# A hybrid decoder step on one core: the state-space input projected first, keys, values and queries beside the state scan

## The reference, cut to what matters

```python
h = rmsnorm(x, g)                      # 1032 tokens together
z = h @ w_in                           # queries 512 | keys/values of three branches 768 | gates 24 | u 512
nsa = gates * (compressed + selected + window attention)   # 8 heads, 2 key heads
state[t] = a * state[t-1] + B u[t]     # complex diagonal state of 32 groups x 64, 1024 steps
y = Re(C state) + d * u;  ssm = gelu(y) * sigmoid(gelu(y) @ glu_w + glu_b)
x = x + norm(concat(norm(nsa), norm(ssm)) @ w_out)
mkv = rmsnorm(mem) @ xkv               # 256 memory tokens: keys and values of the cross-attention
x = x + norm(cross_attention(x, mkv));  x = x + norm(swiglu(x))
```

## Time and profile before

| what | us |
|---|---|
| median of three runs (lowest, highest) | 2453.48 (2452.53, 2455.98) |
| the profiled execution, its own time | 2469.54 |
| its span, first to last instruction | 2467.8 |
| mean granted clock of TensorE over the span, as a share of 2.4 GHz | 0.852 |
| PE busy in the span | 2054.3 |

### The profile page before, as it was taken

One profiled execution on the slowest core, in us unless ns is written; L12 is line 12 of the kernel. 1 busy time (PEld: TensorE's weight loads), 2 busy tenths in 40 slices (PEclk: granted clock), 3 DMA queues, 4 the chain that ended last, 5 costly groups with the idle time before them and its releaser, 6 DMA issues.

```text
span 2467.8 us, 28572 instructions
## 1 busy us (share of the span) xinstructions
PE 2054.3 (83%) x11440; PEld 1758.9 (71%) x11440; DVE 1048.8 (42%) x2439; ACT 625.7 (25%) x1240; POOL 139.3 (6%) x236
## 2 busy tenths in 40 slices
PE   5989890467889889867697879949999999999994
PEld 3646570235778788654497559649999999999993
DVE  3142479939888735200524204081322313223126
ACT  3410120043344444321323113151111111111112
POOL 2100002011101000321000010000000000000000
PEclk9989995675576888966699877969999999999997
DMA  3211112024332100864030030101111111111101
GB/s 120 75 31 35 43 35 77 0 83 134 128 119 95 35 1 1 219 137 105 9 112 26 26 128 1 54 23 35 50 45 46 50 43 50 45 46 50 43 18 77
DMA packets 122547, 151.19 MB, mean 61 GB/s; under 512 B 13488, under 2 KB 104792, under 8 KB 116368
## 3 DMA queue, kind: packets, MB, share of 16 engines
q0 software_dynamic: 17392, 81.67, 10.9%
q1 hardware_dynamic: 95200, 59.91, 8.3%
q10 hardware_dynamic: 9824, 7.78, 1.0%
HBM read 137.03 MB, written 12.31 MB: 61 GB/s over the span
## 4 chain that ended last, share of the span: by engine, by line
PE 46%; DVE 5%; issue 1%; DMA 1%; ACT 1%; POOL 0%; DVEq 0%; POOLq 0%
PE PS L612 43%; PE PS L616 2%; DVE A L2338 1%; DVE A L1766 1%; ACT A L1346 1%; DMA A<-in_cache_mem_kv 1%; DMA A<-new_selected_row 0%; DVE hL L1766 0%; DVE hRaw L1766 0%; DVE A L2349 0%; DVE A L2312 0%; DVE mA L1766 0%; DMA A<-in_norm_g 0%; DVE mS L2314 0%; DVE A L2290 0%
## 5 line engine op out<-in xcount | busy, mean ns | idle before, releaser
L612 PE MATMUL PS<-A 128*128 128x64 f32 (+15 forms) x3728 | 757.7, 365 | 124.8 <-DVEq L2017 86.4
L612 PEld LDWEIGHTS PS<-A 128*128 128x128 f32 (+3 forms) x3728 | 565.8, 211 | 314.8 <-DVEq L2017 86.6
L616 PE MATMUL PS<-ident,A 128*128 128x128 f32 (+9 forms) x1528 | 288.4, 341 | 216.7 <-DVE A L2349 53.8
L616 PEld LDWEIGHTS PS<-ident,A 128*128 128x128 f32 (+9 forms) x1528 | 218.2, 170 | 270.6 <-DVE A L2349 59.8
L1346 ACT ACTIVATE A<-PS 128x256 f32<-128x256 f32 (+15 forms) x404 | 229.8, 586 | 691.6 <-PE PS L612 423.1
L1766 DVE TENSOR_TENSOR A<-A 128x1024 f32<-128x1024 f32 (+11 forms) x405 | 316.5, 785 | 11.4 <-DMA A<-in_cmp_pos 1.4
L612 PE MATMUL PS<-hH,wL 128*128 128x344 f32 x1056 | 224.3, 321 | 2.9 <-issue 2.9
L612 PE MATMUL PS<-hL,wH 128*128 128x344 f32 x1056 | 224.2, 320 | 0.0
L612 PE MATMUL PS<-hH,wH 128*128 128x344 f32 x1056 | 223.6, 320 | 0.0
L612 PEld LDWEIGHTS PS<-hH,wL 128*128 128x128 f32 x1056 | 177.4, 189 | 4.0 <-issue 4.0
L612 PEld LDWEIGHTS PS<-hL,wH 128*128 128x128 f32 x1056 | 177.6, 189 | 0.0
(11 more groups left out here) (265 smaller groups left out, 1798.6 us busy)
## 6 DMA issues: line engine op xcount, KB each, us to landing
wRaw<-in_ffn_wi SPq DMA_DIRECT2D x44, 512.0 KB, 3.8
wRaw<-in_ffn_wo SPq DMA_DIRECT2D x28, 384.0 KB, 3.1
out<-A POOLq DMA_DIRECT2D x16, 512.0 KB, 3.1
A<-in_cache_mem_kv POOLq DMA_DIRECT2D x16, 512.0 KB, 5.0
A<-in_x_prompt SPq DMA_DIRECT2D x8, 512.0 KB, 3.9
A<-in_w_in SPq DMA_DIRECT2D x8, 512.0 KB, 4.1
A<-in_xkv SPq DMA_DIRECT2D x8, 512.0 KB, 3.9
A<-bias_by_distance POOLq DMA_DIRECT2D x8, 512.0 KB, 3.9
```

Source lines behind the costliest of these rows:

```text
L612: return nc.tensor.matmul(out, lhsT=lhsT, rhs=rhs, start=start, stop=stop, skip_group_check=True)
L616: return nc.tensor.transpose(out, in_, ident[b:b + n, b:b + n])
```

## The change

It moves stages; the arithmetic stays. All nine x tiles get buffers of their own and are loaded at once; state and past parameters are issued by SP behind them (the bias table by POOL). `n1` runs for all tiles, with DVE's scaling one tile ahead of its copy. Then come `C`, `h0`, u (m 4 to 7), `SA`/`SB`. DVE's u copies are spread among the building of `CP`. SP loads `wkv` and the weights of the queries when `s5_built` and `u_moved` are set. Then PE does `kv`, `kT`, `cproj`, the queries, and only then waits for the scan; DVE does the value and product work of each kv tile (`kv_rows`) at fixed steps of the scan (`KV_AT`). `bt` units stand between V units from the ninth on; their first two loads are issued behind the kv rows. POOL's first gathers stand behind the last `bt` and `st`. The memory keys and values move behind `glu` 1, ahead of `wT`, with the load of `mem_prompt` issued by ACT at the end of the attention. ACT's list follows PE's. Arena positions are changed to fit.

```diff
+KV_AT = {4: 1, 8: 2, 13: 3, 18: 5, 22: 6, 26: 7}
...
-    order = ["par", ("n1", 0), ("n1", 1)]
-    for i in range(NT + 1):
-        order += [("kv", i)] + ([("n1", i + 2)] if i + 2 <= NT else []) + ([("kT", i - 1)] if i else [])
-    order += ["cproj", "C", "h0"]
-    order += [("in", m, c) for m in range(8) for c in range(2)]
+    order = ["par"] + [("n1", i) for i in range(NT + 1)] + ["C", "h0"]
+    order += [("in", m, c) for m in range(4, 8) for c in range(2)]
     order += [("SA", 0)]
     for j in range(NPAIR):
         order += ([("SA", j + 1)] if j + 1 < NPAIR else []) + [("SB", j)]
-    order += [("mn", i) for i in range(2)] + [("mk", c) for c in range(8)]
-    order += [("V", j) for j in range(NPAIR)]
+    for i in range(NT + 1):
+        order += [("kv", i)] + ([("kT", i - 1)] if i else [])
+    order += ["cproj"]
+    order += [("in", m, c) for m in range(4) for c in range(2)]
+    for j in range(NPAIR):
+        order += [("V", j)] + ([("bt", j - 8)] if j >= 8 else [])
     order += ["ys", "st"] + [("sst", q) for q in range(4)]
-    order += [("bt", h) for h in range(NH)]
...
+    order += [("mn", i) for i in range(2)] + [("mk", c) for c in range(8)]
...
+        for m in (4, 5, 6, 7, 0, 1, 2, 3):
             c0 = m * P if m < 4 else OFF_U + (m - 4) * P
             stream.append((wi_[:, c0:c0 + P], KD, ("in", m, 1)))
+        first_q = 4
+        first_glu = len(stream)
+        for m in range(2):
+            stream.append((glu_w[0][:, m * P:(m + 1) * P], 4, ("glu", m, 1)))
         for m in range(8):
             stream.append((xkv[0][:, m * P:(m + 1) * P], KD, ("mk", m)))
-        first_glu = len(stream)
-        for m in range(4):
...
-                if i >= 2:
-                    full(sp, ("n1", i - 2))
                 src = x_prompt[0, c0:c0 + n, :] if i < NT else x_sample[:, 0, :]
-                sp.dma_start(xin[0:n, i % 2, :], src).then_inc(x_in[i % 2], 16)
-                if i == 1:
+                sp.dma_start(xin[0:n, i, :], src).then_inc(x_in[i], 16)
...
+            def state_parameters():
...
+            def past_parameters():
...
+            for it, (src, kt, _) in enumerate(stream):
+                if it == 2:
+                    state_parameters()
+                if it == NS:
+                    past_parameters()
+                if it == first_q:
+
+                    sp.wait_ge(s5_built, 1)
+                    sp.wait_ge(u_moved, 1)
                     sp.dma_start(wkv, wi_[:, NH * HD:OFF_U].rearrange("(k p) n -> p k n", p=P)).then_inc(wkv_in, 16)
...
-
+                norm_transposes(i)
...
+            dense("in", range(4, 8), [KD], lambda k: hT[:, k])
...
+            pe.wait_ge(wkv_in, 16)
+            for i in range(NT + 1):
+                c0, n = token_tile(i)
+                s = open_(("kv", i))
...
-            for c in range(8):
-                w = next_weights()
...
+            dense("in", range(4), [KD], lambda k: hT[:, k])
...
+                    pe.wait_ge(hank_in[h % 2], 16 * (h // 2 + 1))
+                    s = open_(("bt", h))
+                    for c in range(2):
+                        ins = mm(s[:, c * 512:(c + 1) * 512], flip[:, :], hank[:, h % 2, c * 512:(c + 1) * 512])
+                    ins.then_inc(filled, 1)
             pe.wait_ge(hs_ready, 1)
             s = open_("ys")
             for j in range(NPAIR):
...
             dense("glu", range(2), [4], lambda k: yF[:, k])
 
+            for i in range(2):
...
+            def bias_rows(h):
+                pool.dma_start(hank[:, h % 2], bass.AP(bias_dram.tensor, h * VL, [[1, P], [1, T]]))\
+                    .then_inc(hank_in[h % 2], 16)
+
+            full(pool, ("kv", NT))
+            for h in range(2):
+                bias_rows(h)
...
+            for h in range(2, NH):
+                full(pool, ("bt", h - 2))
+                bias_rows(h)
+
+            full(pool, ("bt", NH - 1))
+            full(pool, "st")
             past_line(0)
...
-            full(act, ("mk", 7))
+
+            for m in range(4):
+                dense_out("in", m, qT[:, m])
             own.settle()
             f(kH, kTd).then_inc(k_hi, 1)
+            for h in range(NH):
+                full(act, ("bt", h))
...
+            full(act, ("PV", n_at - 1))
+            act.dma_start(mrow, mem_prompt[0].rearrange("(i p) d -> p i d", p=P)).then_inc(mem_in, 16)
             for m in range(2):
                 glu_out(m)
+            act.wait_ge(mem_in, 16)
...
+                full(act, ("mk", c))
+                free(f(mkv_new[:, :, c * P:(c + 1) * P], slot(("mk", c))[:, 0:256].rearrange("p (i n) -> p i n", i=2)), ("mk", c))
...
+            act.dma_start(p_mem_kv[0, 0].rearrange("(i p) c h d -> p i (c h d)", p=P), mkv_new).then_inc(mkv_out, 16)
...
+            for i in range(NT + 1):
+                if i < NT:
+                    normalise(i + 1)
+                features(i)
 
...
-            dve.wait_ge(rows_saved, 64)
+            dve.wait_ge(v8_out, 16)
...
+            def states_in(m):
...
+            states_in(0)
+            read_out(dve, "C")
+            for k in range(5):
+                if k == 3:
+                    states_in(1)
+                pw = apow[:, k]
+                cmul(halves(lambda g: CP[:, 0, :, k, 16 * g:16 * g + 16]),
...
+            for m in range(2, 4):
+                states_in(m)
...
+            def kv_rows(i):
+
+                dve.wait_ge(kv_ready, i + 1)
+                own.step(v.tensor_copy(vkeep[:, i].rearrange("p (a c) -> p a c", a=2),
+                                       kvst[:, i % 2, 256:768].rearrange("p (a b c) -> p a b c", a=2, b=2)[:, :, 1]))
+                if i >= 2:
+                    full(dve, ("kT", i - 2))
+                tt(cprod[:, i % 2], kvst[:, i % 2, 0:256], posP).then_inc(prod_ready, 1)
...
+            kv_rows(0)
             for n in range(1, 16):
                 advance(Hm[:, :, n], Hm[:, :, n - 1], 0, 16)
+                if n in KV_AT:
+                    kv_rows(KV_AT[n])
             for m in range(1, 16):
                 advance(Hm[:, m:m + 1, 15], Hm[:, m - 1:m, 15], 1, 1)
+            kv_rows(4)
             for n in range(15):
                 advance(Hm[:, 1:16, n], Hm[:, 0:15, 15], 2 + n, 15)
+                if 16 + n in KV_AT:
+                    kv_rows(KV_AT[16 + n])
 
             sb4 = [P, NPAIR, DB]
...
             dve.sem_inc(hs_ready, 1)
 
-
...
+            dve.wait_ge(kv_stored[0], 16 * (2 * 4 + 2))
+            dve.wait_ge(kv_stored[1], 16 * (2 * 4 + 2))
+            dve.wait_ge(rows_saved, 64)
```

More of the change, by code:

```diff
@@ L407, in hymba_step @@
         params = sem("params")
-        x_in = [sem(f"x_in{s}") for s in range(2)]
+        x_in = [sem(f"x_in{s}") for s in range(NT + 1)]
         wkv_in = sem("wkv_in")
@@ L711, in _ @@
             ins.then_inc(filled, 1)
-            dense("in", range(8), [KD], lambda k: hT[:, k])
+            for i in range(NT - 3, NT + 1):
+                read_out(pe, ("n1", i))
+            dense("in", range(4, 8), [KD], lambda k: hT[:, k])
             def s5_matrices(j):
@@ L1174, in _ @@
             g.memset(eps_c[:, :], EPS).then_inc(consts, 1)
+            with nc.allow_non_contiguous_dma(reason="a table of 32 by 8, transposed"):
+                pool.dma_start(tab[:, :], rel_bias.rearrange("b h -> h b")).then_inc(tab_in, 16)
             pool.wait_ge(params, 16 * PARAM_DMAS)
@@ L1435, in _ @@
-            for part, src in enumerate((state_ssm_re, state_ssm_im)):
-                act.dma_start(h0row[0:DB, part], src[0].rearrange("b g p -> b (g p)")).then_inc(c_in, 16)
-            full(act, "C")
-            for half in range(2):
-                for part in range(2):
-                    s = slot("C")[0:HD, part * 512:part * 512 + 512]\
-                        .rearrange("p (q g i) -> p q g i", g=2, i=16)[:, :, half]
-                    ins = f(cc[64 * half:64 * half + 64, part], s)
-                    free(ins, "C") if half and part else own.step(ins)
@@ L1477, in _ @@
-            act.wait_ge(s5_built, 1)
-            act.dma_start(mrow, mem_prompt[0].rearrange("(i p) d -> p i d", p=P)).then_inc(mem_in, 16)
-            for j in range(NPAIR):
-                s5_out(j)
-                if j == 8:
-                    act.wait_ge(mem_in, 16)
-                    for i in range(2):
-                        own.then(f(junk2, mrow[:, i], ACT.Square, accum_out=st[:, i:i + 1]))
-                        f(st[:, 16 + i:17 + i], st[:, i:i + 1], ACT.Sqrt, scale=1.0 / D, bias=eps_c[:, :]).then_inc(mem_stat, 1)
@@ L1507, in _ @@
             act.sem_inc(states_staged, 1)
-            for h in range(NH):
-                full(act, ("bt", h))
-                free(f(BT[:, h], slot(("bt", h))), ("bt", h))
             def softmax_rows(n, src_ready, stat, x, s, scale=SC):
@@ L2223, in _ @@
                     compressed_branch(key)
+            for i in range(2):
+                dve.wait_ge(mem_stat, i + 1)
```

(6 more changed lines are left out.)

356 lines of the change are left out of this document (159 added, 197 removed).

## The result

The changed kernel takes 2348.84 us (median of four runs, 2340.14 to 2354.44), the kernel before 2453.01 in the same comparison: a ratio of 0.9563, 95% interval 0.9541 to 0.9585. Forecast were 2344, range 2328 to 2370. The profiled execution took 2347.29 us, with a span of 2345.6 and a mean granted clock of 0.879. In the changed file the matmul helper is L651, the transposes L655, ACT's helper L1388, DVE's two-input instructions L1781.

The account below looks back on a forecast made before the run. PE was taken as busy 2054 us, its some 410 us not busy being winnable by reordering. Terms -143.4 ahead of the attention and +33.6 behind it gave -109.8: 2344 us for the median, range 2328 to 2370.

Parts of the forecast that it names:

- Step 1: Start to SA: DVE's serial list of 80.7 us sets the pace, SA at 112.7 against 282.97.
- Step 2: SA, SB, kv, queries: queries begin at 268.4, scan ends by 293 at most, V's first DVE addition at 328.0, 133.5 earlier.
- the crossing: kv and scan lists waiting for each other: costed at nothing, covered by one kv tile, only tile 4 at the edge.
- Step 3: V with bt, to the attention: 4.2 us a pair, then 21.2 us; attention starts at 395.7, 143.4 earlier.
- kL blocks V: Rival in V: `kL` on POOL holds a DVE addition, V's additions 8.6 us later, 2353; chance 0.13.
- Step 4: The attention and its 136 units: unchanged, cost nothing.
- Step 5: Memory keys moved behind the attention: `wT` at 1069.3 instead of 1035.69, 33.6 us added.
- that rival: Memory weights late behind the attention: 1.5 MB more, `mem_prompt` landing only at 1042, 12.5 us added, 2356; chance 0.15.
- The convoy: Rival in kv and scan: mutual waits until the scan runs wholly behind kv, V 58 us later, 2402; chance 0.03.
- the slower rival: PE's clock drops for some 250 us of products moved beside idle stretches, up to 250 more, 2594; chance 0.03.

Follow-up runs that it names:

- the experiment: Eight unused DVE products with both inputs in SBUF added after the first eight V pairs of the changed kernel, beside `kL` on GpSimd: 2363.32 us.
- the second profile of before: The kernel before the change, run and profiled again with no edit: 2449.76 us, its attention 455.2 us.

## Why the prediction was right, step by step

**Step 1 held to 0.1 us, and that is in part luck.** SA at 112.77 for 112.7; u's products end at 92.7 for 92. But the first `hT` copy came 1.0 late (15.46 for 14.5) and a tile took 1.99 for 2.15, which cancels it; DVE's list took 81.3 for 80.7, with 4 us of pauses in it, and SA followed it after 0.2 for 0.8. The mechanism is right: the list of DVE is the bound. Taking 5.3 us out of it moved SA 3.2 earlier, undoing the stagger moved it 16.8 later. The parameters' place behind x instead of ahead of it, which the sum only bounded, is worth 13.5.

**Step 2 has the mis-sized term.** "I cost the crossing at nothing; the cover is one kv tile" was wrong: cproj ends and the queries begin at 276.05 for 268.4. Tiles 1, 2 and 3 were served at 193.0, 204.4 and 218.5, close to the 196, 206 and 219 of the sum; the miss is in "only tile 4 is at the edge, by 1 us": its call for tile 4 lies behind 15 serial steps, 16.4 us in which no rows are served, and its cover of 11.3 is shorter. An edge of 1 us fits a comparison of that call with 234, when the rows of tile 5 are there; but PE comes for row 4 when the products of tile 5 end, 163.1 + 6 x 11.38 = 231.4 by its own period (230.7 measured). PE waited 5.1 us there and 0.9 at the group ahead, and the first tile behind the wait took 12.66 instead of 10.89, at a granted 0.86. Moving that one call gave 5.8 back in this stage, with 2.15 of waiting left at the next group. The scan's end, 277.9 for the 293 of the bound, kept 55 us of distance from the first V product; 8.6 of these 15 are the addition that `kL` no longer holds there.

**Step 3: two terms a little large, one bound not needed.** V and bt take 3.45 us a pair, not 4.2: the durations of merged rows overlap, and the rows start 1.72 apart where I added 2.08 and 1.98. Five pairs and the end of V give back 3.7. From the last V to the attention it was 19.6 for 21.2. That the stores of states behind the gathers end last was right, shown by taking the wait away (6.0 us). So the first score came at 399.28 for 395.7: 7.6 late from step 2, 1.2 more to V's first addition (336.85 for 328.0), 3.7 and 1.6 early.

The rival *kL blocks V* falls, by the experiment and not only by its absence: the lock is there and took 8.32 us from a product with two SBUF inputs, and V's additions, one input in PSUM, passed it at 645 ns at most. This is what the Trainium skill, SBUF — State Buffer, Who interferes with whom, says of two SBUF inputs; these runs agree with it. It also lists `tensor_scalar` among the operations that can contend for the shared ports, when its operands allow it; the 3.65 us beside GpSimd's clearing agree.

**Step 4 was right as far as the spread lets see, and hid a draw in the profile.** No instruction of the attention was changed, yet it was 14.3 us shorter than in the profile of before. The sum was made against that one execution and taken off a median 16 us below it; the second profile of before, 19.8 us shorter, has 17.4 of them in this stage.

**Step 5: 34.8 to 37.0 for 33.6**, by the two profiles of each kernel. In the first, the extra is PE's wait of 3.35 for the second four memory weights, at a DMA share of 0.88. In the second that wait was 0.82 us and the first four took 17.45 for 14.53. `mem_prompt` did not end ACT's wait: it was issued at 860.66, and ACT's first square starts right behind the copy of `glu` 1:

```profile
875.19 1.05 ACT L1388 ACTIVATE A<-A 128x1024 f32<-128x1024 f32 x1
```

So that rival is refuted as to its place, and a small part of its price was paid by the weights instead. The convoy did not form, and PEclk was 0.95 to 0.96 in SA/SB, kv and queries, so the slower rival is out.

In medians the sum was -109.8 for a measured -104.2. The traces have 3.5 of it at the first score, where the crossing cost 8.8 with what followed it and V gave 5.3 back, and 2.7 in the memory stage; what remains is less than what the attention and the part behind `wT` differ by from one execution to the next.

## What to carry to other kernels

When two engines' lists cross at fixed places, compare the longest stretch of one list without a service point with the time that the other can run ahead; an average step says nothing. Here moving one call took most of the wait away. Work that was hidden under one engine's idle time, when that time goes, should look for the next gap before it is put at the end: the memory keys cost 36 us behind the attention and 9 in the gap of 20 us ahead of SA. Before a stage's length is compared between two kernels, profile one of them twice.

## What the runs showed of the hardware

- The same program, executed twice, had stages of 472.7 and 455.2 us, in PE-bound stretches with pauses, with a granted clock of 0.75 and 0.88 over the same 100 us; SA and SB, where PE has no pause, had 0.95 in the kernel before and after.
- A clearing of memory on GpSimd (4.39 us for 5120 columns, where DVE takes 4.33) held a `tensor_scalar` of DVE until it was over (3.65 us for 0.75). A DVE product with an input in PSUM that ran beside it, started 0.04 us ahead of it, kept its 1.22 us.
- A transfer with rows of 16 numbers took 3.4 us to issue on SP behind nine x loads and two of weights, and 0.45 as the first of the queue.
